# Three raw slots and five split slots, in place of five and four, in a streamed-weight kernel

## The reference, cut to what matters

```
c_act = silu(c)
for l in range(2):                       # first block
    sh1, sc1, g1, sh2, sc2, g2 = split(c_act @ ada_w[l] + ada_b[l], 6)
    h = rmsnorm(x, norm1_g[l]) * (1 + sc1) + sh1
    x = x + g1 * token_mix(h, w_in[l], w_fourier[l], w_ret[l], w_out[l])
    h = rmsnorm(x, norm2_g[l]) * (1 + sc2) + sh2
    x = x + g2 * conv_ffn(h, ffn_up[l], conv_w[l], conv_b[l], ffn_down[l])
x = rmsnorm(x, final_g)
# second block: the same frame with attention over windows and over 256 context
# tokens; its layer 2 also carries the context, its layer 3 the 256 tokens alone
```

## Time and profile before

| | |
|---|---|
| median of 2 runs | 2070.65 us (2068.34 to 2072.96) |
| the profiled execution | 2072.03 us, span of its instructions 2070.3 us |
| TensorE busy | 2037.2 us, 98% of the span |
| DVE, ACT, POOL busy | 1514.8, 987.7, 389.5 us |
| mean granted TensorE clock | 0.994 |
| read from memory | 393.08 MB, 190 GB/s over the span |

### The profile page before, as it was taken

One profiled execution on the slowest core, in us unless ns is written; L12 is line 12 of the kernel. 1 busy time (PEld: TensorE's weight loads), 2 busy tenths in 40 slices (PEclk: granted clock), 3 DMA queues, 4 the chain that ended last, 5 costly groups with the idle time before them and its releaser, 6 DMA issues.

```text
span 2070.3 us, 37115 instructions
## 1 busy us (share of the span) xinstructions
PE 2037.2 (98%) x14314; PEld 1872.9 (90%) x14314; DVE 1514.8 (73%) x2169; ACT 987.7 (48%) x1500; POOL 389.5 (19%) x284
## 2 busy tenths in 40 slices
PE   9999999999999999999999999999999999999998
PEld 8999999999999999999877888988888998899998
DVE  7877889977767999978988524898433285876554
ACT  4544456645445465553245533442143254755453
POOL 0421203300601213224101002120020021121120
PEclk9999999999999999999999999999999999999999
DMA  9775767786566656673554322366633244665553
GB/s 329 293 258 198 252 228 253 239 300 223 206 238 220 214 193 217 202 241 125 185 171 143 112 83 98 115 200 224 195 110 102 72 164 143 234 211 173 195 193 105
DMA packets 109739, 396.38 MB, mean 191 GB/s; under 512 B 12424, under 2 KB 13072, under 8 KB 109328
## 3 DMA queue, kind: packets, MB, share of 16 engines
q1 hardware_dynamic: 108304, 389.99, 55.7%
q0 software_dynamic: 1280, 4.20, 0.7%
HBM read 393.08 MB, written 1.05 MB: 190 GB/s over the span
## 4 chain that ended last, share of the span: by engine, by line
PE 79%; DVE 15%; DMA 2%; issue 2%; ACT 1%; POOL 0%; SPq 0%; DVEq 0%; ACTq 0%; POOLq 0%
PE bank L510 19%; PE bank L511 19%; PE bank L512 19%; DVE w_lo L1499 7%; DVE stage L1520 3%; DMA stage<-in_stream 2%; PE bank L708 2%; PE bank L635 2%; PE bank L634 2%; PE bank L633 2%; PE bank L711 2%; DVE conv L1790 1%; DVE conv L1795 1%; DVE rstd L1517 1%; PE bank L534 1%
## 5 line engine op out<-in xcount | busy, mean ns | idle before, releaser
L1499 DVE TENSOR_TENSOR w_lo<-stage,w_hi 128x1024 fp32r<-128x1024 f32 x536 | 716.7, 1352 | 411.0 <-ACT w_hi L1068 409.5
L1068 ACT ACTIVATE w_hi<-stage 128x1024 fp32r<-128x1024 f32 x536 | 566.3, 1060 | 840.3 <-PE bank L512 503.8
L510 PE MATMUL bank<-h_hi,w_hi 128*128 128x256 f32 (+1 forms) x2368 | 721.6, 305 | 8.6 <-DVE w_lo L1499 8.1
L511 PE MATMUL bank<-h_lo,w_hi 128*128 128x256 f32 (+1 forms) x2368 | 716.6, 303 | 0.0
L512 PE MATMUL bank<-h_hi,w_lo 128*128 128x256 f32 (+1 forms) x2368 | 716.4, 303 | 0.0
L510 PEld LDWEIGHTS bank<-h_hi,w_hi 128*128 128x128 f32 x2368 | 445.4, 188 | 37.4 <-DVE w_lo L1499 11.0
L512 PEld LDWEIGHTS bank<-h_hi,w_lo 128*128 128x128 f32 x2368 | 445.3, 188 | 21.5
L511 PEld LDWEIGHTS bank<-h_lo,w_hi 128*128 128x128 f32 x2368 | 445.5, 188 | 21.0
L1520 DVE SCALAR_TENSOR_TENSOR stage<-stage,cvec 128x1024 f32<-128x1024 f32 x192 | 259.9, 1355 | 12.5 <-DMA cols<-in_cols 9.2
L510 PE MATMUL bank<-f_hi,w_hi 128*128 128x256 f32 (+1 forms) x448 | 145.3, 324 | 0.0
L511 PE MATMUL bank<-f_lo,w_hi 128*128 128x256 f32 (+1 forms) x448 | 145.3, 324 | 0.0
(11 more groups left out here) (268 smaller groups left out, 3525.3 us busy)
## 6 DMA issues: line engine op xcount, KB each, us to landing
stage<-in_stream SPq DMA_DIRECT2D x728, 512.0 KB, 4.4
bias<-in_bias POOLq DMA_DIRECT2D x16, 256.0 KB, 3.4
cvec<-in_cvec SPq DMA_DIRECT2D x3, 512.0 KB, 5.1
X<-in_x SPq DMA_DIRECT2D x2, 512.0 KB, 6.1
decay<-in_decay SPq DMA_DIRECT2D x1, 1024.0 KB, 5.5
X<-in_x SPq DMA_DIRECT2D x1, 1024.0 KB, 8.5
out<-X SPq DMA_DIRECT2D x4, 256.0 KB, 2.1
rope<-in_rope SPq DMA_DIRECT2D x2, 256.0 KB, 4.7
```

Source lines behind the costliest of these rows:

```text
L510: mm(out, w_hi[:, slot, w], xh[:, c, 0:T], start=first, stop=False)
L511: mm(out, w_hi[:, slot, w], xl[:, c, 0:T], start=False, stop=False)
L1068: A(w_hi[:, m % NR, :], stage[:, n % NS, :], ACT.Copy).then_inc(hi_ready, 1)
L1499: do(V.tensor_tensor(w_lo[:, m % NR, :], stage[:, n % NS, :], w_hi[:, m % NR, :].bitcast(F32), ALU.subtract), unit_done, done_value(n))
```

## The change

The stream gets three raw slots and five split slots: 3 x 4 + 5 x 8 = 52 KB, as before. The number of loads written out stays 60 (3 x 20). DVE's and ACT's counts at the end of the first norm are adapted to five split slots (`used[0]` 11 in place of 12, and one `advance` more on ACT after it), and the planner, which uses NR, puts mod units one weight unit earlier or later in 136 of the 728 places of the stream: in layer 0's "up" and "dn" steps, in layer 1's "wo" to "up7" and in layer 2's "f1" to "f5".

```
-NS = 5
-NR = 4
+NS = 3
+NR = 5
...
-            FIRST = 12
+            FIRST = 20
             for n in range(FIRST * NS):
                 sp.wait_ge(unit_done, done_value(n))
                 sp.dma_start(stage[:, n % NS, :], t["stream"][n + NS]).then_inc(arrived[n % NS], 16)
...
-                used[0] = 12
+                used[0] = 2 * DC - NR
...
                     act.wait_ge(s["loaded"], 16)
+                    advance(NR - 4)
```

## The result

| | us |
|---|---|
| before, median of 2 runs | 2070.65 |
| after, median of 2 runs | 2231.14 (2229.74 to 2232.53) |
| after / before | 1.0771, interval 1.0749 to 1.0792 |
| forecast | 2121 (2080 to 2160) |

The change costs 160 us, three times the forecast 50, and lies outside the range. Its direction and the place of the cause were forecast, its size not.

The account below looks back on a forecast made before the run. TensorE, busy 98%, was taken as the bound, for some 400 us fed just in time through DVE. The stage terms summed to 50 us, taking the profiled 2072.0 to 2122, so a forecast of 2121 us, range 2080 to 2160.

Parts of the forecast that it names:

- L = 4.2: Every stage: a load's landing time with three raw slots taken as 4.2 us, between 3.3 alone and 5.7.
- The turn of a slot: Every stage: three units pass per landing plus consumers' time, 2.2 us a weight unit and 1.8 a mod unit.
- +13: Layer 0's first step "in", 0 to 69 us: groups of units take 16.1 us instead of 12.45; 13 us added.
- Layer 2: 0: Layer 2: three slots need 5.0 us a weight and mod pair against TensorE's 5.4; nothing added.
- margins of 4 to 12 us lie before TensorE: "k0" to "g1", 69 to 210 us: bursts of units come later, but margins cover them; 0 us added.
- Behind it stand its copies out of PSUM, for which TensorE has eight banks.: ACT's order: it stands longer at landings with copies behind it, but TensorE's eight banks cover that; no cost.
- The up block: Layer 0's "up" steps, 280 to 410 us: each block 1.3 us longer, 12.4 us instead of 11.1 from 355 on.
- +12: Layer 0's last five up blocks and "dn0", 355 to 447 us: 12 us added, less a cushion of 2.76.
- To which the new split slot adds 2.76: Layer 0's first six up blocks: the fifth split slot adds 2.76 us to the feed's 5 us in hand.
- one known gain: TensorE's 14.4 us of waits for split units, all a deeper split buffer can remove; counted as the terms' cushions.
- rival D: Where DVE is full, delays add up between bursts and pauses lower TensorE's clock: 80 to 120 us, 2150 to 2190; chance 0.17.
- B: Only "in" and 355 to 447 us lose, margins take up the bursts elsewhere: 2085 to 2105 us; chance 0.27.

Follow-up runs that it names:

- e10: Kernel before, with only three of its five raw slots in use for the first 28 waits of SP's queue: 2087.83 us, 1.0070.
- e9: Changed kernel, with ACT's copies out of PSUM in af0, af1 and k two units earlier in ACT's order: 2224.84 us, 1.0747.
- e4: Changed kernel, each load bringing half of its unit (256 KB), half of the weights left out: 2151.11 us, 1.0384.
- e8: Changed kernel, each load bringing one eighth of its unit (64 KB), seven eighths left out: 2089.79 us, 1.0084.
- e7: Kernel before with four raw and five split slots, the context's own modulation vector left out: 2111.88 us, 1.0198.
- e11: Four raw and five split slots, context's own vector left out, but ACT and DVE preparing units four ahead: 2099.07 us, 1.0122.
- e1: Kernel before with three raw slots, keeping its four split slots and its order: 2223.78 us, 1.0731.
- e2: Kernel before with four raw slots and its four split slots: 2101.04 us, 1.0147.
- e3: Changed kernel with its five split slots, but an order of four ahead in engines and planner: 2217.44 us, 1.0697.

## Why the prediction was wrong, point by point

**What held.** TensorE alone bounds the kernel, and the split slots had little to give. The landings fell to what I took, L = 4.2 (the earlier trace rows had 5.7 in "in"); windows after, first "in" (34 to 68), then the "up" blocks and "dn0" (406 to 514):

```profile
stage<-in_stream SPq DMA_DIRECT2D x16, 512.0 KB, 4.3
...
stage<-in_stream SPq DMA_DIRECT2D x45, 512.0 KB, 4.2
```

The turn of a slot held where nothing but units is in the way. A group of four mod and four weight units in "in", forecast at 16.1 us, took 16.7: (68.34 - 34.89)/2, against 12.45 in the earlier trace rows.

```profile
34.89 1.23 DVE L1500 TENSOR_TENSOR w_lo<-stage,w_hi 128x1024 fp32r<-128x1024 f32 x1
...
68.34 1.22 DVE L1500 TENSOR_TENSOR w_lo<-stage,w_hi 128x1024 fp32r<-128x1024 f32 x1
```

The term "+13" of "in" measured 14.7 there; with three slots in that step alone (e10) it was 12.7, and 14.5 in the kernel's whole time. "Layer 2: 0" held from behind "v" on (0.1 us in 700).

**The step that failed: the margins between bursts.** "k0" to "g1" at 0, because "margins of 4 to 12 us lie before TensorE", measured 11.8; layer 1 up to "g1", "+3" with "some 8 us in hand", 24.3; "up0" to "up5", "+1", 11.0; layer 2 up to "v", 0, was 13.3; layer 3's attention, "+2", 16.2. These five terms, forecast at 6, measured 76.6 of the 158, while "in" and "ar0" to "wo", where I gave no margin, were 27.6 for 21. I had taken the feed of before as given, late by a few us against a margin of as many units in front of TensorE. What ended TensorE's pauses in these five stretches (us, from the same trace) shows that the margin was counted at the wrong place:

| stretch | added | pauses | by a split unit | by a copy on ACT | by a norm, a residual or other |
|---|---|---|---|---|---|
| "k0" to "g1" | 11.8 | 8.6 | 2.0 | 6.6 | 0 |
| "up0" to "up5" | 11.0 | 10.1 | 4.1 | 0 | 6.0 |
| layer 1, up to "g1" | 24.3 | 17.9 | 6.9 | 8.5 | 2.4 |
| layer 2, up to "v" | 13.3 | 9.6 | 0 | 6.1 | 3.4 |
| layer 3's attention | 16.2 | 12.7 | 0 | 11.2 | 1.5 |

Before, the five had 2.7 us of pauses in all. Only 13 of the 59 us were ended by a unit that wasn't there. All 32 us of waits for ACT's copies lie here. A margin of units in front of TensorE doesn't cover what ACT and DVE do between units: each landing that ACT stands at delays the copies, residuals and norms behind it. e9 shows this for the copies: with them ahead of two units, three of these stretches lost 25 us instead of 49.

In the other stretches up to layer 1's "dn1", where split units ended most of the pauses, the sum of single delays was too small as well: 53 us measured for 23 forecast in "up6" to "dn1" and in layer 1 from "ar0" on. There the question is at which rate a margin is refilled. By the sum's own turn a weight unit with half a mod unit needs 3.1 us against TensorE's 2.76, so what one burst loses isn't won back; with four slots it would need less. That is worked out and agrees with the steep loss from four slots to three, but no run varies the mod units alone. It can't be the cause in the table's fourth stretch: for layer 2 the prediction's sum has the ring at 5.0 us against 5.4, and no split unit ended a pause there. In all stretches together the loss goes with the landing, as e4 and e8 show by dose: 158 us of span at 4.1 us, 82 at 2.9, 17 at 1.9.

**"Behind it stand its copies out of PSUM, for which TensorE has eight banks."** This was a cost put at nothing, and it was about 32 us of waits. ACT's timeline after, 151 to 168 (start, us, what, and the wait before it):

```profile
151.19 0.39 ACT L1189 ACTIVATE v<-bank 128x256 f32<-128x256 f32 x1
...
155.53 1.06 ACT L1068 ACTIVATE w_hi<-stage 128x1024 fp32r<-128x1024 f32 x1 [3.86 <-DMA stage<-in_stream]
157.65 1.06 ACT L1068 ACTIVATE w_hi<-stage 128x1024 fp32r<-128x1024 f32 x1 [1.06 <-DMA stage<-in_stream]
161.25 1.06 ACT L1068 ACTIVATE w_hi<-stage 128x1024 fp32r<-128x1024 f32 x1 [2.55 <-DMA stage<-in_stream]
163.85 1.06 ACT L1068 ACTIVATE w_hi<-stage 128x1024 fp32r<-128x1024 f32 x1 [1.54 <-DMA stage<-in_stream]
164.92 1.28 ACT L1192 ACT_TABLE_LOAD   x1
166.21 1.21 ACT L1192 ACTIVATE y<-bank 128x256 f32<-128x256 f32 x4
```

TensorE's next product starts at 166.65, when that copy had freed a bank; its row is shown under the clock below.

Four landings one behind the other, and a table load of 1.3 us, stand ahead of four short copies, and TensorE has no bank: 6.23 us. Eight banks didn't cover a row of late landings. Such a wait isn't wholly an extra loss: e9 took 18 us of these waits away and won 6.

**The norms** were in no term, and the waits for their sum of squares (`ssum`) grew from 3.5 to 17.5 us. (`h_lo`, 12.3 us, belongs to "in" and its term.) All engines after, at the end of "wo":

```profile
317.12 1.06 ACT L1068 ACTIVATE w_hi<-stage 128x1024 fp32r<-128x1024 f32 x1 [1.56 <-DMA stage<-in_stream]
...
318.21 1.22 DVE L1500 TENSOR_TENSOR w_lo<-stage,w_hi 128x1024 fp32r<-128x1024 f32 x1 [1.40 <-ACT w_hi L1068]
...
319.55 1.66 DVE L1675 SCALAR_TENSOR_TENSOR X<-bank,MOD,X 128x256 f32<-128x256 f32 x4
...
321.89 3.18 POOL L2042 TENSOR_TENSOR ssum<-ssum,sq 128x256 f32<-128x256 f32 x2
...
325.22 1.19 PE L663 MATMUL bank<-ssum,mean_D 128*128 128x256 f32 x2 [5.96 <-POOL ssum L2042]
```

TensorE stops at 319.26 and waits 5.96 us for the sum of squares of that X. From X to TensorE the way by ACT and POOL takes 5.7 us, as it did before (276.44 to 282.13), when TensorE waited 2.22. What is new is where X stands: 0.3 us behind TensorE's last product, where it was 3.5 us ahead of its end. In DVE's order it comes after units whose landings were late, the last of them in the rows above. No run takes this cause away by itself; e7 and e11 show part of it: four ahead instead of five took `ssum` from 11.4 to 4.4.

**The up block**, forecast at 12.4 us, took 428.73 - 415.77 = 13.0 and 442.97 - 428.73 = 14.2, against 11.1 in the earlier trace rows. In the chain of work after:

```profile
421.51 4.87 DMA stage<-in_stream
426.41 1.07 ACT w_hi L1068
427.50 1.23 DVE w_lo L1500
428.73 1.61 DVE conv L1791 x4
...
435.60 5.02 DMA stage<-in_stream
...
442.97 1.61 DVE conv L1791 x4
```

A load of 5 us now stands in the chain once a block, straight ahead of the convolution. I had walked one block with 4.2 and with the units all in when it begins; they aren't, once the block before ended late. With "dn0" (10.8 for 8) the term "+12" became 23.2. Over the whole chain DMA has 18%, where it had 2%, and TensorE 49% for 79%:

```profile
PE 49%; DVE 21%; DMA 18%; ACT 6%; issue 3%; POOL 1%; SPq 0%; DVEq 0%; ACTq 0%; POOLq 0%
```

**"To which the new split slot adds 2.76"**: the cushion wasn't there. (The "one known gain", 14.4 us of waits for split units, was 17.1: one more, of 2.7 us, is in the same view at L708.) By e1 against the change and e2 against e11 the slot is worth about nothing, and its order, five ahead, costs 13 to 14 us in e3 and in e11. Looking further ahead puts more landings in front of ACT's and DVE's other work, as the waits of e7 and e11 show.

**The clock.** Only rival D had it. The granted clock has two levels, 1.2 and 2.4 GHz, which the rows show as 0.50 and 1.00; a mean between them is a mixture. Around the wait of 6.23 us above:

```profile
164.00:170.80 6.80, 4.15 (x19) 4.15 (x20) 4.62 (x9) 5.51 (x8) 0.00 (x0) 0.50 0.80 274
```

```profile
166.65 0.58 PE L510 MATMUL bank<-h_hi,w_hi 128*128 128x256 f32 x1 [6.23 <-ACT y L1192]
167.03 0.41 PE L511 MATMUL bank<-h_lo,w_hi 128*128 128x256 f32 x1
167.24 0.41 PE L512 MATMUL bank<-h_hi,w_lo 128*128 128x256 f32 x1
...
170.86 0.28 PE L511 MATMUL bank<-h_lo,w_hi 128*128 128x256 f32 x1
170.97 0.28 PE L512 MATMUL bank<-h_hi,w_lo 128*128 128x256 f32 x1
```

The clock fell while TensorE stood idle, and came back after 4.2 us of products. At the lower level they start every 0.21 us, at the upper every 0.11. Of the stages shown, those with single pauses of 3.5 to 6 us have a mean of 0.92 to 0.96, the stretch 1183 to 1899 without pauses 1.00; before, 210 to 280 had 1.00.

TensorE's busy time grew by 43.4 us, over a quarter of the loss. Over the whole trace TensorE was busy at the lower level for 70 us, and for 19 before. At half the speed these 51 us more cost some 25, as an estimate. Most of the rest is how busy time counts a pause. A product behind another adds 0.11 us to it, the first after a pause some 0.38; the trace has 83 unbroken stretches of products where it had 31, so 52 x 0.27 = 14 us, as an estimate. All of it fell back with the pauses in e8. No run holds the pauses and takes away the clock alone.

**The rivals.** D named the mechanism, delays that add up from burst to burst, and the clock, but I gave it 0.17 and 120 us at most. B and the forecast both rested on margins. With three slots the stream falls, by the sum's turn, under TensorE's rate wherever every third unit or more is a mod unit: in layer 0 up to "wo" and in its "dn0", and in layer 1 up to the middle of the token mixing.

No version that does the whole work is faster than before. Six raw slots were 4 us under their control, not clear, and need room that the full work doesn't leave; five and four stand.

## What to carry to other kernels

A ring of prefetch slots delivers at most slots over (landing + consumers' time) units per us. Compare this with the use of the bound engine in every stage, those with a margin too, since a margin is only there if the ring is fast enough to refill it. One slot more was worth 123, 30 and 4 us here for the fourth, fifth and sixth, the last not clear of noise. A margin in front of the bound engine says nothing of the others: price what stands behind the late buffer in each in-order engine, copies out of PSUM, residuals and norms, which ended most of the pauses in the stretches that I had put at next to nothing. Looking one unit further ahead behind the late buffer cost 13 to 14 us, and a deeper buffer there won nothing clear.

## What the runs showed of the hardware

- The landing of a load grows with the loads in flight and with its size: in the changed kernel 512 KB had a median of 3.3 us alone, 4.1 with one other in flight and 4.5 with two; before, 5.6 with three others. With three slots 256 KB took 2.9 and 64 KB 1.9. The Trainium skill, "DMA: Bandwidth & Descriptors", section "Anatomy of one DMA", has 2.0 us and the bytes over 436 GB/s, fitted for loads of the other issuing path: as estimates 3.2, 2.6 and 2.2 us for the three sizes. The traces agree within 0.3 us with a load alone and with the smaller ones, and not with 512 KB in company, where the time follows the number in flight.
- Pauses, none over 9.2 us and most under 6, went with a lower granted clock: whole stages had a mean of 0.92 to 0.96, by stretches at 0.50 such as 164 to 170.8, while 406 to 548, with 19 us of pauses of at most 2.3 us each, kept 0.99.
- At the lower level a product of 256 columns took 0.41 us and the next started 0.21 us after it (167.03 and 167.24 above); at the upper level 0.28 and 0.11 (170.86 and 170.97). A long first product after a pause, as the 0.58 us at 166.65, is for the most part this clock: at the upper level the first took some 0.38.
